# Two norms whose rows are transposed by a product with a diagonal of inverse roots

## The chip, the cores and the metric

The kernel runs on one NeuronCore of a Trainium2 chip. The metric is the device time of the core for one execution of the whole program, in microseconds (us). The time before is the median of three runs. The trace and the profile come from one further execution, taken with the hardware profiler.

## The reference, cut to what matters

Two blocks run one after the other on 256 tokens of 1024 columns, in float32. The first has two layers, each a mixer and a mixture of experts (MoE) with a layer norm behind either; the second begins with an RMS norm. What matters here is what stands behind each MoE:

```python
def layer_norm(x, g, b):
    mu = jnp.mean(xf, -1, keepdims=True)
    var = jnp.mean(jnp.square(xf - mu), -1, keepdims=True)
    return (xf - mu) * lax.rsqrt(var + LN_EPS) * g + b
...
    x = layer_norm(ALPHA * x + ffn, ln_ffn_g[l], ln_ffn_b[l])    # layer 0, then attention; layer 1, then second_block
...
def _rmsnorm(x, g):
    return xf * lax.rsqrt(jnp.mean(xf * xf, axis=-1, keepdims=True) + EPS) * g
...
    h = _rmsnorm(x, ln_mix_g[l])
    proj = h @ w_in[l]
```

Behind layer 0 the normed rows are multiplied by `w_kv` (keys and values) and `b_w_q`. Behind layer 1 they are normed once more (RMS) and multiplied by `w_in`.

## The kernel before

**Tiles.** The 256 tokens are two tiles of 128 (`t` in 0, 1), a token to a partition, with 1024 columns in `res`. A product wants its rows transposed: `x_hi` and `x_lo` hold eight chunks of 128 columns by 256 tokens. Every large product is made of three, x_hi·w_hi, x_lo·w_hi and x_hi·w_lo, in a rounded float32 type (`split_product`, L1726). ScalarE rounds the high halves of weights (`high`, L1185) and of rows out of the PSUM banks (`high_T`); VectorE, and at some places GpSimd, subtracts them to make the low halves (`low`, L704; `low_T`, L2642). Weights come through a ring of slots that SP fills, in order, as the slots come free; a block of weights is split in two halves (hb 0 and 1).

**Order.** Each engine has one list of instructions, written out by hand and followed in order; semaphores tell when an engine may go on (`ready`, `freed`, `claim`, `full`, `free` are waits and signals of the banks). GpSimd also issues small DMAs: the rows of gains and shifts and the table of attention bias.

**Behind an MoE** TensorE (PE) makes the last scatter products into four banks, then comes to a branch (L2175) that jumps over the code for experts with more tokens than they have slots for; this code is not taken with these inputs. VectorE adds the banks to `res` (`scattered`, L2983, its additions in L2992) and waits for its own four additions. Then the norm follows:

- `layer_norm_tok` (L2870) on VectorE: statistics of tile 0, then for each tile (row - mean) * gain into `xtok` (L2879), a reciprocal of the root (L2882) and xtok * root + shift (L2884). Gains and shifts are the rows `rows[1][:, 0, :]` and `rows[1][:, 1, :]`, loaded over all partitions.
- `second_tile` (L1206) on ScalarE: mean and variance of tile 1 by two passes with an accumulator, with `xtok` as scratch, and the roots. `root_ahead` (L1200) is a root of a constant that loads the root's table; it stands ahead of `second_tile` (L1391).
- First norm ("ln1", behind layer 0): PE makes two warming products (`warm`, L1720, product L1724) and transposes the rows (`norm_T`, L1927, call L2185, transposes L1936), chunk by chunk, tile 0 first. ScalarE rounds the banks to `x_hi`, VectorE makes `x_lo`, and the product with the first block of keys follows (`keys("k", 0)`, L2239), its first weights split ahead: both high halves by ScalarE at the end of the MoE (L1351), the first low half by GpSimd (L1100) and the second by VectorE behind `low_T` (L721). GpSimd waits for the normed rows (`ln1_tok`) before it loads the attention bias (L1103), since the bias lies where rows were.
- Second norm ("ln3" and then the RMS norm "rm0"): behind `layer_norm_tok` ScalarE squares the rows of each tile with an accumulator (L1521) and takes the root (L1524), VectorE a reciprocal (L2891) and a product (L2892) that writes the scaled rows to `res`, and PE, behind ten warming products, transposes them (call L2353).

The order of the three products in the first block of keys is unit by unit: four output chunks n, each with its three kinds of four products, in a half hb. The first block of the later MLP has a form of its own, `first_hidden` (L2563): all x_hi·w_hi of a half, then all x_lo·w_hi, then all x_hi·w_lo. The PE part `parameters` (L1857) waits for 12 parameter rows, transposes them, then waits for two rows of taps and transposes these. The MoE's experts run as PE L1940, ScalarE L1315, VectorE L2896, with `LAST` the last of eight pairs of experts.

Of the kernel before, what the change touches and what calls it, by code (L numbers as in the profile page):

```python
# [19 lines left out]
F32R = mybir.dt.float32r  # L20
# [5 lines left out]
P = 128  # L26
D = 1024
# [66 lines left out]
def program(nc, a, out):  # L94
    ctx = ExitStack()
    with ctx:
# [139 lines left out]
        parts = choice(NT, P)  # L236
        beats = choice(NG, PER_GROUP, PER_GROUP)
# [130 lines left out]
        ahead = tiny(8)  # L368
# [635 lines left out]
        def _(pool):  # L1004
# [95 lines left out]
            low(pool, g, FIRST_BEHIND[0], 0, pieces=4)  # L1100
# [36 lines left out]
        def _(act):  # L1137
# [68 lines left out]
            def second_tile(n):  # L1206

                at = int(n[2:]) // 2
                act.wait_ge(sem("res_whole"), at + 1)
                s.activation(xtok[:, 1, :], res[:, 1, :], ACT.Identity, accum_out=tile_sum).then_inc(sem("tile_sum"), 1)  # L1210
                std(n, eps_ln, (0,))
                act.wait_ge(sem("tile_sum"), at + 1)
                s.activation(mv[:, 1, 0:1], tile_sum, ACT.Copy, scale=1.0 / D).then_inc(sem("tile_mean"), 1)
                act.wait_ge(sem("tile_mean"), at + 1)
                s.activation(xtok[:, 1, :], res[:, 1, :], ACT.Square, scale=-1.0, bias=mv[:, 1, 0:1],
# [31 lines left out]
            for n in range(2):  # L1247
                par(wst[0:124, n, :], taps[n * 124:(n + 1) * 124, :], "par_taps")
# [66 lines left out]
            def experts(l):  # L1315
# [21 lines left out]
                for u in range(PAIRS):  # L1337
# [4 lines left out]
                    free(copy(hxT[:, 0, :, :], bank(("hT", l, u))[:].rearrange("p (j n) -> p j n", j=4)), ("hT", l, u))  # L1342
                    for r in rs[1:]:
                        gathered(u // 2 + 1, r)
# [6 lines left out]
                highs(FIRST_BEHIND[l])  # L1351
# [21 lines left out]
                with act.If(more > 0):  # L1373
                    over_pairs(act, over_copies)
                with act.Else():
                    act.sem_inc(sem("within"), 1)
# [14 lines left out]
            root_ahead()  # L1391
            second_tile("ln1")
            high_T("ln1")
# [120 lines left out]
            root_ahead()  # L1514
            second_tile("ln3")

# [189 lines left out]
        def _(pe):  # L1706
# [73 lines left out]

            def linear_tok(name, label, cols=HALF, i=0, **more):
# [75 lines left out]
            def parameters():  # L1857

                pe.wait_ge(sem("par_rows"), 16 * 12)
# [4 lines left out]
                pe.wait_ge(sem("par_taps"), 16 * 2)  # L1864
# [62 lines left out]
            def norm_T(name, src=res, made="xhat", before=0):  # L1927
# [257 lines left out]
            norm_T("ln1", xtok, "tok", 2)  # L2185
# [53 lines left out]
            keys("k", 0, arrives="ln1")  # L2239
# [1320 lines left out]
```

## Time and profile before

| what | value |
|---|---|
| median of three runs | 1200.62 us (1198.33 to 1203.09) |
| the profiled execution, its own time | 1205.38 us |
| its span in the trace | 1203.70 us |
| mean granted clock of TensorE, as a share of full speed | 0.989 |
| busy share of the span | PE 95%, weight load 66%, VectorE 53%, ScalarE 38%, GpSimd 19% |
| chain that ended last | PE 65%, VectorE 20%, DMA 5%, ScalarE 4%, issue 3% |

PE is TensorE's products and PEld its weight loads, which lie beside them; DVE is VectorE, ACT ScalarE, POOL GpSimd, SP SyncE. A name like L2992 is a line of the kernel. The chain is followed back from the last instruction, at each step to what released it; "issue" in it is time in which the engine waited for nothing that the profile shows. A row of a timeline gives start, busy time, engine, line, operation, output and inputs with their shapes, and in brackets how long the engine had been idle and what ended that.

### The profile page before, as it was taken

Reading aid. Unit: us, or ns where it says so; the run is one execution under the profiler, and the core shown is the slowest. Engines: PE = TensorE matmul, PEld = TensorE weight load, DVE = VectorE, ACT = ScalarE, POOL = GpSimd, SP = SyncE. Lnnn points to the kernel's source line nnn. Section 1 sums busy time; section 2 is a strip of 40 time slices with the busy share of each in tenths; the row PEclk is TensorE's granted clock in tenths of the full one; section 3 lists DMA queues with packets and bytes.
Section 4 is the critical chain, followed back from the end, with each engine's and each line's share of the span. In section 5 each row is a group of like instructions: output and inputs, shape, how many; then the busy total and the mean of one; then the engine's idle time right before and its main releaser. Section 6 shows DMA issues by size and latency. Waiting matters only on the chain.

```text
span 1203.7 us, 16471 instructions
## 1 busy us (share of the span) xinstructions
PE 1141.1 (95%) x6682; PEld 793.6 (66%) x6682; DVE 642.6 (53%) x969; ACT 453.5 (38%) x663; POOL 229.6 (19%) x198
## 2 busy tenths in 40 slices
PE   8999999999879998899999898999999889999998
PEld 8967544444239976444444347889887768998997
DVE  4897542222145767542222145873699885545544
ACT  4434411111034565411111025574566534443442
POOL 6500100000020000000000000586798541000000
PEclk9999999999989999999999999999999999999999
DMA  9497999999986447999999976443333342553550
GB/s 321 144 319 281 392 399 421 421 421 421 421 315 193 142 174 283 391 386 422 420 421 421 421 289 214 159 153 140 140 140 140 140 140 71 219 202 139 210 209 36
DMA packets 87222, 321.66 MB, mean 267 GB/s; under 512 B 7208, under 2 KB 18917, under 8 KB 62571
## 3 DMA queue, kind: packets, MB, share of 16 engines
q1 hardware_dynamic: 84336, 313.08, 67.3%
q0 software_dynamic: 2256, 7.30, 2.0%
q8 instruction: 54, 0.88, 0.3%
q10 hardware_dynamic: 554, 0.22, 0.1%
q14 instruction: 22, 0.17, 0.0%
HBM read 318.63 MB, written 1.96 MB: 266 GB/s over the span
## 4 chain that ended last, share of the span: by engine, by line
PE 65%; DVE 20%; DMA 5%; ACT 4%; issue 3%; POOL 2%; SPq 1%; DVEq 0%; ACTq 0%
PE bank L1764 30%; PE bank L2017 16%; PE bank L2087 8%; DMA arena<-in_moe_w_up_dram 5%; DVE w_lo L721 3%; ACT w_hi L1146 2%; PE bank L2099 2%; POOL w_lo L721 2%; DVE arena L2705 1%; PE bank L2008 1%; PE bank L2571 1%; PE bank L1808 1%; DVE arena L3020 1%; DVE arena L3364 1%; DVE rows L3345 1%
## 5 line engine op out<-in xcount | busy, mean ns | idle before, releaser
L1146 ACT ACTIVATE w_hi<-ring 128x2048 fp32r<-128x2048 f32 (+2 forms) x103 | 192.3, 1871 | 187.8 <-PE bank L1764 177.6
L721 DVE TENSOR_TENSOR w_lo<-ring,w_hi 128x2048 fp32r<-128x2048 f32 x71 | 161.9, 2282 | 135.2 <-ACT w_hi L1146 135.2
L721 POOL TENSOR_TENSOR w_lo<-ring,w_hi 128x512 fp32r<-128x512 f32 (+1 forms) x124 | 178.8, 1474 | 81.2 <-ACT w_hi L1146 81.2
L2017 PE MATMUL bank<-ring,moe_x 128*64 128x512 f32 x336 | 104.0, 610 | 7.4 <-DMA arena<-in_moe_w_up_dram 6.0
L1146 ACT ACTIVATE arena<-bank 128x512 f32<-128x512 f32 (+5 forms) x70 | 33.6, 492 | 203.9 <-PE bank L2074 184.3
L1764 PE MATMUL bank<-x_hi,w_hi 128*128 128x256 f32 (+1 forms) x616 | 101.8, 287 | 1.7 <-issue 1.7
L1764 PE MATMUL bank<-x_hi,w_lo 128*128 128x256 f32 (+1 forms) x616 | 99.4, 284 | 2.6 <-POOL w_lo L721 1.4
L1764 PE MATMUL bank<-x_lo,w_hi 128*128 128x256 f32 (+1 forms) x616 | 99.0, 283 | 0.5 <-DVE x_lo L2656 0.4
L1764 PE MATMUL bank<-w_hi,x_hi 128*128 128x512 f32 x320 | 91.7, 400 | 7.4 <-DVE x_lo L2787 2.9
L1764 PE MATMUL bank<-w_lo,x_hi 128*128 128x512 f32 x320 | 89.5, 393 | 4.2 <-POOL w_lo L721 3.5
L2981 DVE TENSOR_TENSOR y_r<-bank,y_r 128x512 fp32r<-128x512 f32 x32 | 22.1, 692 | 133.2 <-ACT y_r L1146 133.2
L1764 PE MATMUL bank<-w_hi,x_lo 128*128 128x512 f32 x320 | 88.7, 391 | 0.1
L1764 PEld LDWEIGHTS bank<-x_hi,w_hi 128*128 128x128 f32 (+1 forms) x616 | 84.5, 191 | 3.9 <-issue 3.3
L1764 PEld LDWEIGHTS bank<-x_hi,w_lo 128*128 128x128 f32 (+1 forms) x616 | 84.7, 191 | 3.2 <-POOL w_lo L721 1.8
L1764 PEld LDWEIGHTS bank<-x_lo,w_hi 128*128 128x128 f32 (+1 forms) x616 | 84.5, 191 | 1.1 <-issue 1.1
L2017 PE MATMUL bank<-arena,moe_x 128*64 128x512 f32 x240 | 82.5, 615 | 0.0
L3020 DVE SCALAR_TENSOR_TENSOR arena<-arena,small,bank 128x512 f32<-128x512 f32 x16 | 18.1, 1131 | 118.7 <-PE bank L2017 118.7
L1062 POOL DMA_DIRECT2D rows<-in_ln_ffn_g_dram x2 | 1.1, 536 | 392.8 <-DMA arena<-in_moe_w_down_dram 392.8
L2017 PEld LDWEIGHTS bank<-ring,moe_x 128*64 128x64 f32 x336 | 32.2, 140 | 65.7 <-issue 65.7
L1764 PEld LDWEIGHTS bank<-w_lo,x_hi 128*128 128x128 f32 x320 | 59.3, 188 | 20.4 <-POOL w_lo L721 7.0
L1764 PEld LDWEIGHTS bank<-w_hi,x_hi 128*128 128x128 f32 x320 | 58.2, 189 | 20.6 <-DVE x_lo L2787 3.8
L1764 PE MATMUL bank<-w_hi,mhT 128*128 128x512 f32 x256 | 70.1, 395 | 0.0
(409 smaller groups left out, 1827.4 us busy)
## 6 DMA issues: line engine op xcount, KB each, us to landing
ring<-in_moe_w_gate_dram SPq DMA_DIRECT2D x30, 1024.0 KB, 16.1
ring<-in_w_in_dram SPq DMA_DIRECT2D x15, 2048.0 KB, 7.6
arena<-in_moe_w_up_dram SPq DMA_DIRECT2D x26, 1024.0 KB, 19.1
arena<-in_moe_w_gate_dram SPq DMA_DIRECT2D x24, 1024.0 KB, 15.0
ring<-in_moe_w_up_dram SPq DMA_DIRECT2D x24, 1024.0 KB, 18.7
arena<-in_moe_w_down_dram SPq DMA_DIRECT2D x24, 1024.0 KB, 17.3
wslots<-in_moe_w_down_dram SPq DMA_DIRECT2D x24, 1024.0 KB, 21.4
ring<-in_w_mlp_up_dram SPq DMA_DIRECT2D x8, 2048.0 KB, 8.5
```

The lines of the kernel that those rows point to most:

```text
L721: last = ops.tensor_tensor(part(w_lo, label, hb)[:, x].bitcast(F32R), ring_half(label, hb)[:, x], part(w_hi, label, hb)[:, x], ALU.subtract)
L1146: return s.activation(dst, src, ACT.Copy)
L1764: last = mm(bank(use_)[0:still.shape[1], at:at + cols], still, moving, start=start and opens and (hb, n, k) == (0, 0, 0), stop=stop and cl ...
L1808: last = mm(bank(use_)[:, n % 2 * T:n % 2 * T + T], w_[hb][:, k, n * P:(n + 1) * P], x_[:, 4 * hb + k, :].bitcast(F32R), start=opens and n ...
L2008: last = mm(b[:, i * width:(i + 1) * width], rows_[:, t, c * P:(c + 1) * P].bitcast(F32R), sel[:, t, :].bitcast(F32R), start=(n, t) == (0, ...
L2017: last = mm(b[half * CAP:(half + 1) * CAP, :], still(k)[:, half * CAP:(half + 1) * CAP], moving(half, k), start=k == 0, stop=k == k_range - 1)
L2087: last = mm(bank(("y", l, u, h))[half * CAP:(half + 1) * CAP, :], hxT[:, 0, j, half * CAP:(half + 1) * CAP], down_rows(("down", l, 2 * u + ...
L2099: last = mm(b, sel_T[:, buf, t * P:(t + 1) * P].bitcast(F32R), y[:, h * HALF:(h + 1) * HALF].bitcast(F32R), start=n == 0, stop=n == 1)
L2571: last = mm(bank((*label, n // 2))[:, n % 2 * T:n % 2 * T + T], w_[hb][:, k, n * P:(n + 1) * P], x_[:, 4 * hb + k, :].bitcast(F32R), start ...
L2705: ins = v.scalar_tensor_tensor(conv[:, c, :], hpad[:, c, j:j + T], wdw[:, j * KD + c:j * KD + c + 1], conv[:, c, :], ALU.mult, ALU.add)
L2981: return v.tensor_tensor(y_lo[:, cols].bitcast(F32R), b, y_hi[:, cols], ALU.subtract)
L3020: free(v.scalar_tensor_tensor(hidden_rows(hx[:, 0, :]), by_hidden(sg[:, 0, :]), slot_gates[:, u % 2, :], by_hidden(bank(("up", l, u))[:]), ...
```

## The change

- **The two transposes.** `norm_T` gives way to `scaled_T`: a chunk of rows is not transposed as such but multiplied, in float32, by a diagonal matrix of inverse roots, so that the chunk comes out transposed and scaled. The diagonals lie in `scale_T` (the memory of `parts`), made by VectorE from the identity (`diagonal`). In the first norm the rows multiplied are (row - mean) * gain, and the shift comes into the banks before them, by 16 products of the shift's row with the identity that need nothing of the norm. One warming product in place of two goes ahead of these; in the second norm nine in place of ten.
- **The normed rows of the first norm**, which later work reads, are written behind the products' rows by `times_root`; GpSimd's wait for them stays.
- **VectorE's order.** It no longer waits for all four of the last additions together (`scattered`): tile 0's statistics wait for its own two banks, tile 1's product for the others. In the second norm both first products come ahead of both roots.
- **ScalarE's order.** `second_tile` waits for the banks instead of a signal of VectorE and uses `x_lo` as scratch. The root's table is asked for at the last pair of experts, behind the copy of `hT`; in the path for overfull experts it is asked for again. The second half of the split of the first weights goes behind `second_tile`.
- **The first low half** of the keys' weights goes from GpSimd to VectorE, behind `layer_norm_tok`.
- **The first block of keys** is multiplied in passes: `first_hidden` becomes `in_passes`, used for both.
- **Parameters and taps** count on one semaphore, waited for once.

```diff
+        scale_T = parts
...
-        ahead = tiny(8)
+        ahead = tiny(10)
...
-            low(pool, g, FIRST_BEHIND[0], 0, pieces=4)
             for t in range(NT):
                 pool.wait_ge(sem("ln1_tok"), t + 1)
             load_bias(0, bias1)
...
             def second_tile(n):
 
-                at = int(n[2:]) // 2
-                act.wait_ge(sem("res_whole"), at + 1)
-                s.activation(xtok[:, 1, :], res[:, 1, :], ACT.Identity, accum_out=tile_sum).then_inc(sem("tile_sum"), 1)
+                l = int(n[2:]) // 2
+                unread = x_lo[:, 0:4, :].rearrange("p c t -> p (c t)").bitcast(F32R)
+                for h in range(2):
+                    freed(act, ("sc", l, LAST, 1, h))
+                s.activation(unread, res[:, 1, :], ACT.Identity, accum_out=tile_sum).then_inc(sem("tile_mean"), 1)
+                act.wait_ge(sem("tile_mean"), 2 * l + 1)
+                s.activation(mv[:, 1, 0:1], tile_sum, ACT.Copy, scale=1.0 / D).then_inc(sem("tile_mean"), 1)
                 std(n, eps_ln, (0,))
-                act.wait_ge(sem("tile_sum"), at + 1)
-                s.activation(mv[:, 1, 0:1], tile_sum, ACT.Copy, scale=1.0 / D).then_inc(sem("tile_mean"), 1)
-                act.wait_ge(sem("tile_mean"), at + 1)
-                s.activation(xtok[:, 1, :], res[:, 1, :], ACT.Square, scale=-1.0, bias=mv[:, 1, 0:1],
+                act.wait_ge(sem("tile_mean"), 2 * l + 2)
+                s.activation(unread, res[:, 1, :], ACT.Square, scale=-1.0, bias=mv[:, 1, 0:1],
                              accum_out=mv[:, 1, 1:2]).then_inc(sem("ln_var"), 1)
...
-                par(wst[0:124, n, :], taps[n * 124:(n + 1) * 124, :], "par_taps")
+                par(wst[0:124, n, :], taps[n * 124:(n + 1) * 124, :], "par_rows")
...
+                    if u == LAST:
+                        root_ahead()
...
-                highs(FIRST_BEHIND[l])
+                high(FIRST_BEHIND[l], 0)
...
                     over_pairs(act, over_copies)
+                    root_ahead()
+                    act.wait_ge(sem(f"over_steps{l}"), 4 * PAIRS * (ROUNDS - 1))
...
             experts(0)
-            root_ahead()
             second_tile("ln1")
+            high(FIRST_BEHIND[0], 1)
             high_T("ln1")
...
+            def in_passes(label, arrives):
...
+                for hb in range(2):
+                    pe.wait_ge(hi_made[hb], nth_split(label) + 1)
+                    pe.wait_ge(sem("x_hi"), ROUNDED[arrives] + 2 * (hb + 1))
+                    for n in range(4):
+                        products(n, x_hi, wh, hb, opens=not hb)
+                    for b in (2 * hb, 2 * hb + 1):
+                        freed(pe, (arrives, b))
+                    for n in range(4):
+                        products(n, x_lo, wh, hb)
+                    pe.wait_ge(lo_made[hb], nth_split(label) + 1)
+                    for n in range(4):
+                        last = products(n, x_hi, wl, hb, closes=bool(hb))
+                        if n == 0:
+                            last.then_inc(hi_read[hb], 1)
+                        if hb and n % 2:
+                            full(last, (*label, n // 2))
+                    if not hb:
+                        last.then_inc(lo0_read, 1)
...
-                pe.wait_ge(sem("par_rows"), 16 * 12)
+                pe.wait_ge(sem("par_rows"), 16 * 14)
-                pe.wait_ge(sem("par_taps"), 16 * 2)
...
+            def scaled_T(name, before, shifted=False):
+
+                warm((name, 0), before)
+                for b in range(4):
+                    if b:
+                        claim(pe, (name, b))
+                    for c in (2 * b, 2 * b + 1) if shifted else ():
+                        for t in range(NT):
+                            at = c % 2 * T + t * P
+                            mm(bank((name, b))[:, at:at + P], rows[1][:, 1, c * P:(c + 1) * P], ident[:],
+                               start=(c % 2, t) == (0, 0), stop=False)
+                for t in range(NT):
+                    pe.wait_ge(sem("rows_scale"), NT * ("ln1", "rm0").index(name) + t + 1)
+                    for b in range(4):
+                        for c in (2 * b, 2 * b + 1):
+                            at = c % 2 * T + t * P
+                            last = mm(bank((name, b))[:, at:at + P], xtok[:, t, c * P:(c + 1) * P], scale_T[:, t, :],
+                                      start=not shifted, stop=not shifted or (c % 2, t) == (1, NT - 1))
+                        if t == NT - 1:
+                            full(last, (name, b))
...
             experts(0)
-            norm_T("ln1", xtok, "tok", 2)
+            pe.wait_ge(sem("rows1"), 32)
+            scaled_T("ln1", 1, shifted=True)
...
-            keys("k", 0, arrives="ln1")
+            in_passes(("k", 0), "ln1")
...
-            norm_T("rm0", before=10)
+            scaled_T("rm0", 9)
...
+            def times_root(n, t):
+                r = rows[1]
+                dve.wait_ge(sem(f"{n}_xhat"), t + 1)
+                v.scalar_tensor_tensor(xtok[:, t, :], xtok[:, t, :], rstd[:, t, 1:2], r[:, 1, :], ALU.mult, ALU.add)\
+                    .then_inc(sem(f"{n}_tok"), 1)
+            def diagonal(t):
+                v.tensor_scalar(scale_T[:, t, :], ident[:], rstd[:, t, 1:2], None, ALU.mult).then_inc(sem("rows_scale"), 1)
             def layer_norm_tok(n):
-                r = rows[1]
-                dve.wait_ge(sem("rows1"), 32 * (int(n[2:]) // 2 + 1))
-                for t in range(NT):
-                    if t == 0:
-                        half_stats(t, 0).then_inc(sem("res_whole"), 1)
-                        moments(n, t, half_stats(t, 1))
-                    dve.wait_ge(sem("ln_var"), NT * int(n[2:]) + t + 1)
+                l, r = int(n[2:]) // 2, rows[1]
+                dve.wait_ge(sem("rows1"), 32 * (l + 1))
+                def less_mean_gained(t):
                     v.scalar_tensor_tensor(xtok[:, t, :], res[:, t, :], mv[:, t, 0:1], r[:, 0, :], ALU.subtract, ALU.mult)\
                         .then_inc(sem(f"{n}_xhat"), 1)
+                def root(t):
                     dve.wait_ge(sem("ln_std"), NT * int(n[2:]) + t + 1)
                     link(v.reciprocal(rstd[:, t, 1:2], rstd[:, t, 0:1]))
-                    dve.wait_ge(sem(f"{n}_xhat"), t + 1)
-                    v.scalar_tensor_tensor(xtok[:, t, :], xtok[:, t, :], rstd[:, t, 1:2], r[:, 1, :], ALU.mult, ALU.add)\
-                        .then_inc(sem(f"{n}_tok"), 1)
-            def rms_norm(n):
+                    if n == "ln1":
+                        dve.wait_ge(sem(f"{n}_xhat"), t + 1)
+                        diagonal(t)
+                    else:
+                        times_root(n, t)
+                for h in range(2):
+                    freed(dve, ("sc", l, LAST, 0, h))
+                    last = half_stats(0, h)
+                moments(n, 0, last)
+                dve.wait_ge(sem("ln_var"), NT * int(n[2:]) + 1)
+                less_mean_gained(0)
+                if n == "ln1":
+                    root(0)
+                dve.wait_ge(sem("tile_mean"), 2 * l + 2)
+                for h in range(2):
+                    freed(dve, ("sc", l, LAST, 1, h))
+                less_mean_gained(1)
+                if n == "ln3":
+                    root(0)
+                root(1)
+            def rms_scale():
                 for t in range(NT):
                     dve.wait_ge(sem("rms_std"), t + 1)
                     link(v.reciprocal(rstd[:, t, 1:2], rstd[:, t, 0:1]))
-                    v.tensor_scalar(res[:, t, :], xtok[:, t, :], rstd[:, t, 1:2], None, ALU.mult)\
-                        .then_inc(sem(f"{n}_xhat"), 1)
+                    diagonal(t)
...
-                    for t in range(NT):
+                    for t in range(NT if u < LAST else 0):
...
             layer_norm_tok("ln1")
+            low(dve, v, ("k", 0), 0)
             low_T("ln1")
             low(dve, v, ("k", 0), 1)
+            for b in range(4):
+                ready(dve, ("ln1", b))
+            for t in range(NT):
+                times_root("ln1", t)
...
             layer_norm_tok("ln3")
-            rms_norm("rm0")
+            rms_scale()
```

## Rows read from the trace of the kernel before

**Rows 1.** Page, parts 1 and 3: busy time by engine; DMA queue 8, its packets, MB and share.

```profile
PE 1141.1 (95%) x6682; PEld 793.6 (66%) x6682; DVE 642.6 (53%) x969; ACT 453.5 (38%) x663; POOL 229.6 (19%) x198
...
q8 instruction: 54, 0.88, 0.3%
```

**Rows 2.** Chain of waits, 338 to 396 us: start us, us, what.

```profile
351.52 5.28 issue
356.80 3.75 PE bank L1724 x4
```

**Rows 3.** Line L2175: count, durations in ns (min/median/max), first and last start in us.

```profile
L2175 PEldq COMPARE_BRANCH  x2: 429/3344/6260, 350.4 to 712.8; - x2
```

**Rows 4.** DMA queues, 353.9 to 355.3 us: packets, MB, share of 16 engines.

```profile
q8 instruction: 1, 0.02, 4.9%
```

**Rows 5.** Windows: PE, PEld, DVE, ACT, POOL busy us (instructions), PE clock, DMA share, GB/s.

```profile
354.90:358.20 3.30, 1.40 (x2) 0.84 (x3) 3.27 (x3) 2.56 (x7) 2.41 (x2) 0.50 0.41 152
...
361.70:363.70 2.00, 1.31 (x12) 1.10 (x11) 0.71 (x2) 1.40 (x6) 1.30 (x2) 1.00 0.18 66
```

**Rows 6.** Timelines of VectorE and ScalarE, first norm: start us, us, instruction, idle before.

```profile
353.05 1.28 DVE L2663 BATCH_NORM_STATS2 stats<-res 128x6 f32<-128x512 f32 x2 [0.45 <-DVE res L2992]
...
359.70 1.28 DVE L2884 SCALAR_TENSOR_TENSOR xtok<-xtok,rstd,rows 128x1024 f32<-128x1024 f32 x1
...
362.30 2.32 ACT L1146 ACTIVATE x_hi<-bank 128x256 fp32r<-128x256 f32 x8 [4.78 <-PE bank L1936]
...
365.39 2.28 DVE L721 TENSOR_TENSOR w_lo<-ring,w_hi 128x2048 fp32r<-128x2048 f32 x1
```

**Rows 7.** Timeline of PE, second norm.

```profile
713.89 8.85 PE L1724 MATMUL bank<-blockmask,ident 128*128 128x512 f32 x20
```

**Rows 8.** Chain of waits, 700 to 752 us.

```profile
714.35 0.69 DVE res L2992
...
721.03 1.29 DVE xtok L2884
...
723.86 0.17 DVE rstd L2891
...
724.06 1.13 DVE res L2892
...
725.71 0.85 ACT x_hi L1154 x2
```

**Rows 9.** Line L2494: its PE instructions, and its first sixteen in the timeline.

```profile
L2494 PE MATMUL bank<-arena x128: 270/275/377, 843.6 to 940.8; 128*128 128x128 f32 x128
...
843.62 2.05 PE L2494 MATMUL bank<-arena 128*128 128x128 f32 x16 [1.12 <-DVE small L3352]
```

**Rows 10.** Timeline of PE, first norm.

```profile
360.34 2.57 PE L1936 MATMUL bank<-ident,xtok 128*128 128x128 f32 x16
...
363.61 0.71 PE L1764 MATMUL bank<-x_hi,w_hi 128*128 128x256 f32 x4 [0.69 <-issue]
...
364.42 0.71 PE L1764 MATMUL bank<-x_lo,w_hi 128*128 128x256 f32 x4
...
364.97 0.64 PE L1764 MATMUL bank<-x_hi,w_lo 128*128 128x256 f32 x4
```

**Rows 11.** Groups by line and form, VectorE: out<-in xcount | busy us, mean ns | idle before.

```profile
L3240 DVE TENSOR_SCALAR arena<-rows,small 128x128 f32<-128x128 f32 x1 | 0.3, 286 | 0.0
```

**Rows 12.** Timeline of ScalarE, first norm.

```profile
345.45 0.60 ACT L1146 ACTIVATE y_r<-bank 128x512 fp32r<-128x512 f32 x1 [3.90 <-PE bank L2087]
...
351.18 1.91 ACT L1146 ACTIVATE w_hi<-ring 128x2048 fp32r<-128x2048 f32 x1
353.10 1.28 ACT L1202 ACT_TABLE_LOAD   x1
```

**Rows 13.** DMA issues, 340 to 365 us: count, KB each, median us to landing.

```profile
arena<-bias_lines POOLq DMA_DIRECT2D x1, 1024.0 KB, 6.6
```

**Rows 14.** Timeline of VectorE, 389 to 392 us.

```profile
390.93 0.42 DVE L3087 SCALAR_TENSOR_TENSOR arena<-bank,arena 128x256 f32<-128x256 f32 x1
```

More of the change, by code:

```diff
@@ L1513, in _ @@
             experts(1)
-            root_ahead()
             second_tile("ln3")
+            high(FIRST_BEHIND[1], 1)
             def mean_square(n, arrived, of):
@@ L1779, in split_product, with products @@
                         last.then_inc(sem(blocks[label]["read"]), 1)
+            def in_passes(label, arrives):
+                wh, wl = ([part(w, label, hb).rearrange("p (k n) -> p k n", n=HALF).bitcast(F32R) for hb in range(2)]
+                          for w in (w_hi, w_lo))
+                def products(n, x_, w_, hb, opens=False, closes=False):
+                    for k in range(4):
+                        last = mm(bank((*label, n // 2))[:, n % 2 * T:n % 2 * T + T], w_[hb][:, k, n * P:(n + 1) * P],
+                                  x_[:, 4 * hb + k, :].bitcast(F32R), start=opens and (n % 2, k) == (0, 0),
+                                  stop=closes and (n % 2, k) == (1, 3))
+                    return last
+                for b in range(2):
+                    claim(pe, (*label, b))
+                for hb in range(2):
[16 more added lines that the diff above has]
+                        last.then_inc(lo0_read, 1)
             def linear_tok(name, label, cols=HALF, i=0, **more):
@@ L2561, in _ @@
             rows_T(1)
-            def first_hidden():
-                label = ("mu", 0)
-                wh, wl = ([part(w, label, hb).rearrange("p (k n) -> p k n", n=HALF).bitcast(F32R) for hb in range(2)]
-                          for w in (w_hi, w_lo))
-                def products(n, x_, w_, hb, opens=False, closes=False):
-                    for k in range(4):
-                        last = mm(bank((*label, n // 2))[:, n % 2 * T:n % 2 * T + T], w_[hb][:, k, n * P:(n + 1) * P],
-                                  x_[:, 4 * hb + k, :].bitcast(F32R), start=opens and (n % 2, k) == (0, 0),
-                                  stop=closes and (n % 2, k) == (1, 3))
-                    return last
-                for b in range(2):
-                    claim(pe, (*label, b))
-                for hb in range(2):
-                    pe.wait_ge(hi_made[hb], nth_split(label) + 1)
-                    pe.wait_ge(sem("x_hi"), ROUNDED["rm1"] + 2 * (hb + 1))
-                    for n in range(4):
-                        products(n, x_hi, wh, hb, opens=not hb)
-                    for t in range(NT):
-                        freed(pe, ("rm1", 2 * hb + t))
-                    for n in range(4):
-                        products(n, x_lo, wh, hb)
-                    pe.wait_ge(lo_made[hb], nth_split(label) + 1)
-                    for n in range(4):
-                        last = products(n, x_hi, wl, hb, closes=bool(hb))
-                        if n == 0:
-                            last.then_inc(hi_read[hb], 1)
-                        if hb and n % 2:
-                            full(last, (*label, n // 2))
-                    if not hb:
-                        last.then_inc(lo0_read, 1)
             OUT_ORDER = [(0, 0), (0, 1), (1, 0), (1, 1), (0, 2), (1, 2), (0, 3), (1, 3)]
@@ L2602, in mlp @@
                 if first:
-                    first_hidden()
+                    in_passes(("mu", 0), "rm1")
                 else:
@@ L2993, in scattered @@
                         free(ins, ("sc", l, u, t, h))
-                    for t in range(NT):
+                    for t in range(NT if u < LAST else 0):
                         for h in range(2):
```

## The prediction

> **What bounds the kernel now.** TensorE (PE) does: it is busy for 95% of the span [rows 1], so a norm between two stages costs what PE loses at it. I therefore read the chain of waits around the two norms that change, then each engine's timeline there.
>
> *First norm (behind the first MoE layer).* The reader should see that PE is not waiting for the norm when the stage begins. Its last scatter product ends at 351.52, and 5.28 us pass that the chain calls issue: PE waited for nothing that the profile shows. Two warming products and the transposes follow [rows 2]. The branch at L2175, which jumps over the code for overfull experts, says what it was: it took 6.26 us the first time and 0.43 us the second [rows 3]. Meanwhile a block of some 16 KB (54 blocks hold 0.88 MB) came over the instruction queue [rows 1, 4]. So this is a wait for code. Behind it the granted clock was 0.50 (1.2 GHz of 2.4), and at 361.7 it was back at 1.00 [rows 5]. VectorE's second tile ended at 359.70 + 1.28 = 360.98, and ScalarE began to round the new rows at 362.30 [rows 6].
>
> *Second norm (ahead of the second block).* Here PE's ten warming products run without a gap [rows 7], and the chain alternates between VectorE and ScalarE, from the end of the last addition at 715.04 to the first rounding at 725.71 [rows 8].
>
> By the Trainium skill's page Runtime: NRT & Kernel Launch, section Instruction fetch mechanics, a taken branch to a target outside the loaded window has to fetch that block first; the two times of this one branch agree with that.
>
> **The change, part by part.** Times are of the profiled execution: 1205.38 us, with a span of 1203.70. That is 4.8 us over the median of the three runs, 1200.62; the sum is made on the first and moved to the second.
>
> *The wait for code stays.* Ahead of that branch PE's program loses one wait at most (parameters and taps share a semaphore now), so branch and target move by one instruction out of some 250 in a block (6682 products, as many weight loads, 54 blocks [rows 1]). I take the 6.26 us as unchanged: PE begins at 356.80 as before.
>
> *What PE then does in the first norm.* Before: two warming products and 16 transposes. Now: one warming product, 16 float32 products that put the shift into the banks, 16 that multiply by the diagonal. A float32 product is two records: L2494's 64 products are 128. Sixteen records take 2.05 us, the last of them 0.28, so one starts every (2.05 - 0.28) / 15 = 0.118 us at full clock [rows 9], and every 0.236 at half. Warming: two records of (360.34 - 356.80) / 4 = 0.885 us [rows 2, 10], to 358.6. Shift: 32 records; 13.3 of them at half clock until 361.7, 18.7 more in 2.2 us, to 363.9. Tile 0: 16 records, 1.89 us, to 365.8. The first bank is whole after four records of tile 1, 3 x 0.118 + 0.28 = 0.63 us, at 366.4, where ScalarE begins instead of at 362.30: **+4.1 us**. The clock sets both ends: full speed throughout gives 356.80 + 0.89 + 3.78 + 1.89 + 0.63 = 364.0 (+1.7), half speed to the end 370.9 (+8.6). I take the value between, since up to 356.80 PE's history is that of rows 5.
>
> By the Trainium skill's page TensorE: Matmul & The Clock Gate, section Terms, transpose mode is four times faster for FP32; by that a product would cost four transposes and the first norm would lose some 7 us more. The rows show two records a product, and the sum goes by them.
>
> *What VectorE and ScalarE save there is covered.* VectorE begins its statistics with the end of the last addition, not 0.45 us later [rows 6], and no longer runs beside GpSimd's splitting. A multiply-add over 1024 columns gives way to a diagonal of 128 columns. The trace has no such diagonal; its ends are the 0.17 us reciprocal and the 1.13 us multiplication of 1024 columns [rows 8], and I take 0.29, a multiplication of 128 columns in SBUF [rows 11], as nearest. The second scale is then made at about 357.5, where the second tile was whole at 360.98. PE, which wants it at 365.8, hides all of that; without the wait for code it would count (rival 1).
>
> *Moved steps at no cost.* The root's table (1.28 us) goes into ScalarE's idle 3.90 us that end at 345.45; the second half of the split (1.91 us) goes behind the statistics, into the 4.78 us before 362.30 [rows 6, 12]. The low half of the first weight block passes from GpSimd to VectorE: 2.28 us [rows 6] between 357.5 and 366.4, where VectorE has nothing else; were PE ready at 358.8, the first low part of the rows would come 1 us late, which 16 products cover. The normed rows are written behind the products, 2 x 1.28 us on VectorE, whose next split has to wait for PE's last reading of the block and for ScalarE; without that cover, 2.6 us. GpSimd waits for these rows before it issues the bias load, which goes from 361 to about 374 and with 6.6 us in flight [rows 13] lands by 381; the row of shifts behind it in GpSimd's queue is read a layer later. The bias is first read at 390.93 [rows 14], and now later by the same shift: 10 us are left. SP's next weight load wants the low half read, and moves with PE. The joined wait for parameters and taps comes two small transposes earlier for the taps: 0.3 us at most, once.
>
> *First block in passes.* The same products in another order. The first group of four to the second took 0.81 us, against 0.55 for the next [rows 10]: **-0.3 us**, as the low part is wanted only after 16 products.
>
> *Second norm.* Statistics begin 0.45 us earlier. The new order (both first products, then both roots) has tile 0's rows whole at 720.5 and tile 1's at 721.9, where the latter were whole at 721.03 + 1.29 = 722.3. Square, sum and root took from there to 723.86, 1.54 us, and now end at 723.4; then a reciprocal (0.17) and a diagonal (0.29) stand for a reciprocal and a 1.13 us multiplication [rows 8], and the second scale is there at 723.9, not 725.2. But PE has tile 0 first: by the same steps its scale comes at 722.4, and 16 records take 1.89 us, to 724.3; then 0.63 us for the first bank: 724.9 against 725.71. **-0.8 us** (0 to -1.0 by the ends for the diagonal). What is late next is PE, no longer VectorE. Nine warming products instead of ten end before that.
>
> *Sum:* 4.1 - 0.3 - 0.8 = **+3.0 us**: 1208.4 for the profiled execution, **1203.6 us** on the median. What follows a norm shifts with it, the next MoE layer's loads too: SP issues them in order, as slots come free.
>
> **Rivals.**
> 1. *The wait for code goes* (the target is loaded in time, as at the second norm). PE then starts at 351.6 at full clock: 0.87 + 3.78 to 356.3, tile 0 to 358.2, the first bank at 358.8, and ScalarE begins 3.5 us earlier. With -0.3 and -0.8 that is -4.6: 1196.0 us. For it: the same branch took 0.43 us once [rows 3]. Against it: a single wait moves ahead of that branch. It decides where the first branch takes under some 2 us.
> 2. *The second branch gets a wait for code* (slower). Behind the first branch PE's program grows by 92 instructions (33 products of four against two of four and 16 transposes of two), so the second branch lies elsewhere in its block. Its price: 6.26 - 0.43 = 5.8 us, so warming starts at 719.7, at half clock; of 18 records 5.5 take 4.9 us, the rest 12.5 x 0.44 = 5.5 us, to 730.1; with 1.89 and 0.63 the first bank is whole at 732.6, 6.9 us late instead of 0.8 early. In all 4.1 - 0.3 + 6.9 = +10.7: 1211.3 us. It decides where the second branch takes over some 3 us. For it: the first branch. Against it: this jump once passed with room, and 92 of 250 need not use that up. By the section of the Trainium skill named above, Instruction fetch mechanics, it depends on nothing but the block in which the target falls.
> 3. *The clock stays at half* through the first norm's products: 8.6 - 0.3 - 0.8 = +7.5, 1208.1 us. Rows 5 speak against it.
>
> A table loaded again at the join behind the branch would change nothing: it was there before and is not in the chain of either norm.
>
> **How the numbers follow.** The forecast has 0.75, with 1201 to 1207 of its own by the clock; rival 1 has 0.13, rival 2 0.05, rival 3 0.04; 0.03 is left for what I don't see. A measurement of this kernel can tell about 0.5%, 6.0 us, from no change: faster is under 1194.6, slower over 1206.6. Rival 1 alone comes near the first, and with the runs' own spread of 2.4 us either way less than half of its chance falls below it; rivals 2 and 3 and the forecast's upper edge make slower. Faster 0.06, no change 0.81, slower 0.13. The range takes in the forecast with its clock and the runs' spread, and half of rival 1: 1196 to 1208.
>
> **What would show it.** Right: L2175 takes some 6 us first and under 1 us the second time; PE idles from 351.5 to 356.8 and then works without a gap through 64 records into about 366; VectorE has made the second scale before 358; ScalarE's first rounding falls at 366 in the first norm, and in the second 9.9 us behind the last addition (10.7 before). Wrong: a first rounding before 361, a long second branch, records of a product at other than 0.11 to 0.12 us.

## The result: 0.4% slower, and the profile after

| | before | after |
|---|---|---|
| median of six runs each | 1201.45 us (1198.33 to 1203.09) | 1207.76 us (1204.78 to 1209.28) |
| ratio | | 1.0042, 95% interval 1.0026 to 1.0058: 5.0 us slower (3.1 to 7.0) |
| profiled execution, its span | 1205.38, 1203.70 us | 1206.18, 1204.5 us |
| first norm: end of the last scatter product to ScalarE's first rounding | 351.52 to 362.30: 10.78 us | 350.70 to 364.96: 14.26 us |
| block of keys: its first product to that of the next block | 363.61 to 375.53: 11.92 us | 366.31 to 377.89: 11.58 us |
| second norm: end of the last addition to the first rounding | 715.04 to 725.71: 10.67 us | 717.23 to 728.93: 11.70 us |

The medians lie 6.3 us apart and the ratio on record makes it 5.0; its interval takes in both. The three stretches give +3.48, -0.34 and +1.03: +4.2 us, inside the interval too. The two profiled executions differ by 0.8 us only. In other stretches, with the same instructions in both, the granted clock fell at different places: from 97 to 100 us it was 0.50 after and 1.00 before, which cost PE some 1.6 us, and behind 1017 us it was the other way round, for 1.5 us. So the stretches are compared here, and the runs for the sum.

Busy time of the engines, part 1 of the page after [rows 1 of before]:

```profile
PE 1143.4 (95%) x6742; PEld 799.5 (66%) x6742; DVE 643.3 (53%) x972; ACT 453.5 (38%) x663; POOL 222.5 (18%) x194
```

PE has 60 records more: 46 in the first norm (66 against 20) and 14 in the second (50 against 36).

**First norm.** The branch's line, then the chain of waits of the kernel after [rows 2, 3]:

```profile
L2233 PEldq COMPARE_BRANCH  x2: 343/3385/6427, 349.6 to 715.0; - x2
```

```profile
350.70 5.60 issue
356.30 2.04 PE bank L1730 x2
358.34 4.34 PE bank L1986 x32
362.69 3.57 PE bank L1993 x32
366.26 0.05 issue
366.31 11.74 PE bank L1794 x96
```

The wait for code is there as before, 6.43 us at the first branch. Behind it PE works without a gap through one warming product (two records), 32 records of shift and 32 of rows. ScalarE begins to round when PE has filled the first bank (its timeline after):

```profile
364.96 2.32 ACT L1146 ACTIVATE x_hi<-bank 128x256 fp32r<-128x256 f32 x8 [8.15 <-PE bank L1993]
```

VectorE had both diagonals at 354.93 and 356.52, long before PE turned to the rows at 362.69 (its timeline after):

```profile
354.64 0.29 DVE L2905 TENSOR_SCALAR arena<-ident,rstd 128x128 f32<-128x128 f32 x1
...
356.23 0.29 DVE L2905 TENSOR_SCALAR arena<-ident,rstd 128x128 f32<-128x128 f32 x1
...
370.25 2.48 DVE L2900 SCALAR_TENSOR_TENSOR xtok<-xtok,rstd,rows 128x1024 f32<-128x1024 f32 x2
```

The windows of the kernel after give the clock [rows 5; columns as there]:

```profile
353.00:356.30 3.30, 0.00 (x1) 0.03 (x1) 3.19 (x7) 3.24 (x7) 0.00 (x0) 0.50 1.03 377
356.30:359.80 3.50, 3.50 (x10) 2.46 (x11) 2.42 (x2) 0.51 (x1) 0.00 (x0) 0.50 0.42 157
359.80:364.96 5.16, 5.16 (x48) 5.16 (x47) 0.00 (x0) 0.00 (x1) 0.00 (x0) 1.00 0.01 1
```

It fell while PE stood at the branch and was back 3.5 us behind PE's start; before, that took 361.7 - 356.8 = 4.9.

**Second norm.** VectorE's timeline after, then GpSimd's:

```profile
724.33 1.91 DVE L2905 TENSOR_SCALAR arena<-ident,rstd 128x128 f32<-128x128 f32 x1
725.52 0.72 DVE L2944 RECIPROCAL rstd<-rstd 128x1 f32<-128x1 f32 x1
726.30 0.29 DVE L2905 TENSOR_SCALAR arena<-ident,rstd 128x128 f32<-128x128 f32 x1
```

```profile
724.27 0.91 POOL L1098 DMA_DIRECT2D arena<-bias_lines  x1 [8.56 <-DVE xtok L2900]
725.18 0.97 POOL L1116 MEMSET arena<- 128x1024 f32 x1
```

The same instruction that took 0.29 us three times takes 1.91 here, and its end, 726.24, lies 0.09 us behind that of GpSimd's clearing (726.15). PE waits for it, and ScalarE for PE (their timelines, after):

```profile
716.09 7.99 PE L1730 MATMUL bank<-blockmask,ident 128*128 128x512 f32 x18
726.38 3.85 PE L1993 MATMUL bank<-arena,xtok 128*128 128x128 f32 x32 [2.30 <-DVE arena L2905]
...
728.93 3.03 ACT L1154 ACTIVATE x_hi<-bank,pcol 128x256 fp32r<-128x256 f32 x8 [3.44 <-PE bank L1993]
```

### The profile page after: what moved, and what is told of

It is laid out like the page before. It is cut to its first block, busy times and chain, and to the rows that moved or that the text cites. A ratio compares the mean times of both kernels' runs of the same rounds, so it can differ in the third digit from the quotient of the medians.

```text
span 1204.5 us, 16593 instructions
## 1 busy us (share of the span) xinstructions
PE 1143.4 (95%) x6742; PEld 799.5 (66%) x6742; DVE 643.3 (53%) x972; ACT 453.5 (38%) x663; POOL 222.5 (18%) x194
## 4 chain that ended last, share of the span: by engine, by line
PE 67%; DVE 17%; DMA 5%; ACT 4%; issue 3%; POOL 3%; SPq 0%; DVEq 0%; ACTq 0%
PE bank L1770 31%; PE bank L2075 16%; PE bank L2145 8%; DVE w_lo L722 3%; POOL w_lo L722 3%; DMA arena<-in_moe_w_down_dram 2%; DMA arena<-in_moe_w_up_dram 2%; ACT w_hi L1146 2%; PE bank L2157 2%; PE bank L1794 2%; DVE arena L2731 1%; DVE arena L3072 1%; PE bank L1846 1%; PE bank L2066 1%; DVE rows L3402 1%
## 5 line engine op out<-in xcount | busy, mean ns | idle before, releaser
L722 DVE TENSOR_TENSOR w_lo<-ring,w_hi 128x2048 fp32r<-128x2048 f32 (+1 forms) x72 | 164.1, 2282 | 131.9 <-ACT w_hi L1146 131.4
L722 POOL TENSOR_TENSOR w_lo<-ring,w_hi 128x512 fp32r<-128x512 f32 (+1 forms) x120 | 173.1, 1475 | 68.5 <-ACT w_hi L1146 68.5
L2075 PE MATMUL bank<-ring,moe_x 128*64 128x512 f32 x336 | 101.1, 600 | 7.9 <-DMA arena<-in_moe_w_up_dram 6.0
L1770 PE MATMUL bank<-x_hi,w_hi 128*128 128x256 f32 x584 | 96.6, 287 | 0.4 <-issue 0.4
L1770 PE MATMUL bank<-x_hi,w_lo 128*128 128x256 f32 x584 | 94.2, 284 | 2.6 <-POOL w_lo L722 1.4
L1770 PE MATMUL bank<-x_lo,w_hi 128*128 128x256 f32 x584 | 93.7, 283 | 0.3 <-DVE x_lo L2682 0.3
L1770 PEld LDWEIGHTS bank<-x_hi,w_lo 128*128 128x128 f32 x584 | 80.3, 191 | 3.2 <-POOL w_lo L722 1.8
L1770 PEld LDWEIGHTS bank<-x_hi,w_hi 128*128 128x128 f32 x584 | 80.1, 191 | 2.2 <-issue 1.7
L1770 PEld LDWEIGHTS bank<-x_lo,w_hi 128*128 128x128 f32 x584 | 80.1, 190 | 0.8 <-issue 0.8
L2075 PE MATMUL bank<-arena,moe_x 128*64 128x512 f32 x240 | 79.6, 601 | 0.0
```

Of the source, the lines that this page charges most:

```text
L722: last = ops.tensor_tensor(part(w_lo, label, hb)[:, x].bitcast(F32R), ring_half(label, hb)[:, x], part(w_hi, label, hb)[:, x], ALU.subtract)
L1770: last = mm(bank(use_)[0:still.shape[1], at:at + cols], still, moving, start=start and opens and (hb, n, k) == (0, 0, 0), stop=stop and cl ...
L2075: last = mm(b[half * CAP:(half + 1) * CAP, :], still(k)[:, half * CAP:(half + 1) * CAP], moving(half, k), start=k == 0, stop=k == k_range - 1)
```

## The experiments

Each kernel's norms are measured as in the table above. The kernel before has one more trace, that of before_clear_behind: its first norm, untouched there, took 10.00 us instead of 10.78. So one pair of traces doesn't show a difference under 1 us in the first norm. The second norm of the changed kernel (11.66 or 11.70 us in the five traces that leave its clearing as it is and have a short second jump) and its block of keys (11.58 or 11.59 in all eight traces with the passes) agree much better.

| kernel | ratio to before (95%) | median or single run, us | first norm | second norm |
|---|---|---|---|---|
| after | 1.0042 (1.0026 to 1.0058) | 1207.76 | 14.26 | 11.70 |
| after_placed | 0.9985 (0.9971 to 1.0000) | 1201.65 | 7.50 | 11.66 |
| before_placed | 1.0004 (0.9990 to 1.0018) | 1202.61 | 10.25 | 10.67 |
| after_no_shift | 1.0009 (0.9994 to 1.0023) | 1203.36 | 10.98 | 11.66 |
| after_second_far | 0.9999 (0.9986 to 1.0012) | 1201.19 | 6.97 | 15.37 |
| after_bias_behind | 1.0019 (1.0006 to 1.0032) | 1205.48 | 13.94 | 10.07 |
| after_clear_behind | single run | 1205.57 | 13.98 | 10.07 |
| before_clear_behind | single run | 1203.13 | 10.00 | 10.32 |
| after_units | single run | 1208.02 | 15.29 | 11.66 |
| placed_table_back | single run | 1200.93 | 7.74 | 11.66 |
| after_both | 0.9979 (0.9964 to 0.9993) | 1200.05 | 7.78 | 10.04 |

### The wait for code taken away, from either kernel

```diff
-            warm(("pw2", 0, 0), 4)
+            warm(("pw2", 0, 0), 18, cols=P)
...
                 with pe.If(more > 0):
+                    for _ in range(100 if l == 0 else 0):
+                        pe.sem_inc(sem("within"), 1)
```

after_placed has both edits on the kernel after, before_placed the first on the kernel before.

> The changed kernel with its program moved: 56 more instructions ahead of PE's first branch (18 short warming products ahead of the second convolution product instead of 4 long ones, in PE's idle time there) and 100 that are never executed behind it, so that both jumps land at other places of the program. Theory (the wait for code makes the first norm slower): both jumps take under 1 us, PE starts the warming product at most 0.5 us behind the last scatter product instead of 5.60 us, the 16 shift products end before the first diagonal, and ScalarE's first rounding falls 6.8 to 7.3 us behind the last scatter product instead of 14.26: some 7 us less, 1199 to 1201. Rival (the products themselves are the price): the first rounding stays over 10 us behind, and the time over 1203. Rival (the clock): PE works, but at half clock until the rounding, 9 to 11 us behind, 1202 to 1204.

> The kernel before with the same 56 instructions ahead of PE's first branch. Theory: the first jump takes under 1 us too, but VectorE's second tile (whole 9.46 us behind the last scatter product) then sets the end: first rounding 9.8 to 10.3 us behind instead of 10.78, 0.5 to 1 us less, about 1200.7. Rival (the wait for code cost the kernel before as much as the changed one): 5 us less, about 1196.

The branch's line in after_placed, then its timeline of PE:

```profile
L2233 PEldq COMPARE_BRANCH  x2: 404/430/455, 351.8 to 710.5; - x2
```

```profile
351.83 1.16 PE L2157 MATMUL bank<-y_r,selT_r 128*128 128x512 f32 x4 [0.37 <-DVE y_r L3035]
353.02 1.10 PE L1730 MATMUL bank<-blockmask,ident 128*128 128x512 f32 x2
353.95 3.73 PE L1986 MATMUL bank<-ident,rows 128*128 128x128 f32 x32
357.52 0.39 PE L1993 MATMUL bank<-arena,xtok 128*128 128x128 f32 x2
358.18 3.62 PE L1993 MATMUL bank<-arena,xtok 128*128 128x128 f32 x30 [0.27 <-issue]
```

Both jumps are short, and PE goes on 0.02 us behind its last scatter product. It turns from the shift to the rows at 357.52, and the first diagonal is there at 357.23, so PE and VectorE are about level. The norm takes 7.50 us instead of 14.26, and the ratio falls by 0.0057, 6.8 us: theory and size hold, though the time, 1201.65 us, lies a little over the 1199 to 1201 expected. The windows of the norm show a clock of 1.00 throughout:

```profile
353.00:353.90 0.90, 0.88 (x2) 0.47 (x3) 0.90 (x2) 0.00 (x0) 0.00 (x0) 1.00 1.05 382
353.90:357.50 3.60, 3.60 (x33) 3.55 (x32) 3.50 (x8) 3.27 (x8) 0.00 (x0) 1.00 0.96 354
357.50:360.50 3.00, 2.73 (x24) 2.54 (x23) 2.96 (x4) 1.60 (x2) 0.00 (x0) 1.00 0.14 46
```

In before_placed both jumps took under 0.46 us too, but PE then waits for VectorE (its timeline of PE):

```profile
351.41 1.98 PE L1724 MATMUL bank<-blockmask,ident 128*128 128x512 f32 x4
358.50 1.94 PE L1936 MATMUL bank<-ident,xtok 128*128 128x128 f32 x8 [5.10 <-DVE xtok L2884]
361.00 1.97 PE L1936 MATMUL bank<-ident,xtok 128*128 128x128 f32 x8 [0.56 <-DVE xtok L2884]
```

It idles 5.10 us, and the granted clock, back at 1.00 from 361.7 on in the kernel before, is 0.50 here from 358.4 until 367.0 (windows of before_placed):

```profile
363.03:367.00 3.97, 3.97 (x18) 3.97 (x19) 3.97 (x5) 2.50 (x6) 0.00 (x0) 0.50 0.88 316
367.00:372.00 5.00, 5.00 (x43) 5.00 (x43) 0.10 (x1) 1.58 (x1) 0.00 (x0) 1.00 0.92 287
```

The norm takes 10.25 us, which lies between the two traces of the kernel before (10.00 and 10.78), the block of keys behind it takes 13.34 instead of 11.92, and the time is that of the kernel before, not the 0.5 to 1 us less that were expected. So the old norm hid the wait for code behind VectorE, and the new one, which relieves VectorE and gives PE more to do, stands on it. Without that wait the change is worth 2.75 us in this norm, and in these two traces 1.75 more in the block of keys (13.34 to 11.59), most of it by the clock.

By the Trainium skill's page Runtime: NRT & Kernel Launch, section Instruction fetch mechanics, a taken branch waits for a fetch when its target lies outside the part of the program that is loaded. The four jumps of these two kernels agree: they took 0.32 to 0.46 us, with only the number of instructions ahead of them or skipped by them changed.

### The other branch made the far one

```diff
-                    for _ in range(100 if l == 0 else 0):
+                    for _ in range(20 if l == 0 else 0):
```

> As after_placed, but with 20 never executed instructions behind the first jump instead of 100, so that the second jump, and not the first, should land beyond the part of the program that is loaded. Theory (the wait for code goes by the place of a jump in the program alone): the first jump takes under 1 us and the second some 6 us; in the second norm PE's 18 warming records then begin about 5.5 us late and at half clock, and the first rounding falls about 17 us behind the last addition instead of 11.7; the time is 5 to 6 us over after_placed, 1206 to 1208. Rival (the second jump is always short, since more time lies before it): as after_placed.

The branch's line and the chain of waits of the second norm:

```profile
L2233 PEldq COMPARE_BRANCH  x2: 460/2345/4230, 347.3 to 705.4; - x2
```

```profile
706.54 3.26 issue
709.80 10.92 PE bank L1730 x18
720.72 2.25 PE bank L1993 x20
```

Against after_placed, where both jumps are short, eighty never executed instructions fewer bring a wait to the second jump; against the kernel after, the edits move the wait from one norm to the other. The jump took 4.23 us rather than 6, and the norm 15.37 us rather than 17. The time expected, 1206 to 1208 us, was missed: it was 1201.19. Against after_placed the two norms give +3.7 - 0.5 = 3.2 us; the ratio rose by 0.0014, 1.7 us, and each of the two ratios is uncertain by as much. That the wait goes by place is shown; why it was 2 us shorter here stays open.

### The shift left out

```diff
-            pe.wait_ge(sem("rows1"), 32)
-            scaled_T("ln1", 1, shifted=True)
+            scaled_T("ln1", 1)
```

This leaves the shift out of the rows from which keys, values and queries are made.

> The changed kernel without the 16 products that put the shift into the banks (the rows that the keys, values and queries are made of lack the shift). Theory (PE's list behind the wait for code sets the end of the first norm): PE idles 5.6 us as before, then 2 + 32 records, and the first rounding is 3 to 4.3 us earlier than 14.26 us behind the last scatter product; 3 to 4 us less. Rival (VectorE and ScalarE set the end): nothing changes.

The norm is 3.3 us shorter (14.26 to 10.98) and the ratio falls by 0.0033, 4.0 us. Behind its wait for code PE's own list is the path.

### GpSimd's work moved behind the diagonals

```diff
             pool.wait_ge(sem("ln3_tok"), NT)
+            pool.wait_ge(sem("rows_scale"), 2 * NT)
             load_bias(1, bias2)
```

In after_clear_behind the new wait stands behind `load_bias`, ahead of the clearing; in before_clear_behind it stands there too, on the scaled rows (`rm0_xhat`).

> The changed kernel, with one more wait on GpSimd: the second bias load and the clearing behind it wait for both diagonals of the second norm. Theory (GpSimd's load and clearing held up VectorE's first diagonal): that diagonal takes 0.29 us instead of 1.91 for the pair's first, the first rounding of the second norm falls 10.0 to 10.3 us behind the last addition instead of 11.7, and the time is 1.6 us less. Rival (the diagonal behind a reciprocal is itself so long there, or waits for ScalarE): it stays at over 1.5 us and nothing changes.

> The changed kernel with GpSimd's clearing (0.97 us) alone behind both diagonals of the second norm; the bias load stays ahead of them. If the load's issue (0.91 us on GpSimd, begun 0.06 us before the first diagonal) holds VectorE up as well, that diagonal ends with the issue, after 0.9 to 1.2 us; if the clearing alone does, it takes 0.29 us.

> The kernel before with GpSimd's clearing behind the second scaled rows of the second norm. Theory (the clearing held VectorE up there too, only less): the product of 1024 columns for the second tile takes 0.75 us, as the first tile's did, instead of 1.12, and the first rounding falls 10.3 us behind the last addition instead of 10.67. Rival (the second tile's product is itself longer): 1.12 us still.

VectorE and GpSimd in after_clear_behind (their timelines):

```profile
724.18 0.28 DVE L2906 TENSOR_SCALAR arena<-ident,rstd 128x128 f32<-128x128 f32 x1
...
725.57 0.29 DVE L2906 TENSOR_SCALAR arena<-ident,rstd 128x128 f32<-128x128 f32 x1
```

```profile
724.13 0.91 POOL L1098 DMA_DIRECT2D arena<-bias_lines  x1 [8.56 <-DVE xtok L2901]
725.92 0.95 POOL L1117 MEMSET arena<- 128x1024 f32 x1 [0.88 <-DVE arena L2906]
```

With the bias load beside it and the clearing behind, the first diagonal takes 0.28 us; the norm takes 10.07 us in both kernels, 1.63 less. So it is the clearing, not the load's issue. In the old kernel it cost 0.37: with the clearing behind, the second product took 0.75 us instead of 1.12, and the norm 10.32 instead of 10.67.

The lines of the kernel before, VectorE and GpSimd, then VectorE in before_clear_behind:

```profile
722.42 0.75 DVE L2892 TENSOR_SCALAR res<-xtok,rstd 128x1024 f32<-128x1024 f32 x1
...
724.06 1.12 DVE L2892 TENSOR_SCALAR res<-xtok,rstd 128x1024 f32<-128x1024 f32 x1
```

```profile
723.66 0.97 POOL L1116 MEMSET arena<- 128x1024 f32 x1
724.68 0.56 POOL L1118 MEMSET arena<- 128x16 f32 x1
```

```profile
721.82 0.75 DVE L2893 TENSOR_SCALAR res<-xtok,rstd 128x1024 f32<-128x1024 f32 x1
...
723.46 0.75 DVE L2893 TENSOR_SCALAR res<-xtok,rstd 128x1024 f32<-128x1024 f32 x1
```

It looks as if the hold goes both ways: beside the end of the long product GpSimd's second, small clearing took 0.56 us, and 0.12 us in before_clear_behind, where VectorE had nothing beside it. No run tried this by itself.

The ratio of after_bias_behind, 0.0023 under that of after (2.8 us), agrees with 1.63 us within the intervals.

### Two steps that were to cost nothing, or little

```diff
-            in_passes(("k", 0), "ln1")
+            keys("k", 0, arrives="ln1")
```

> The changed kernel with the first block of keys unit by unit again. Theory: from its first product to the first of the next block 11.9 us instead of 11.58, the first four products being followed by a gap until the first low part is there; 0.3 us more, too little for the time of a run. Rival: the passes make no difference, 11.6 us.

Unit by unit the block takes 11.92 us (367.04 to 378.96), as before; the passes are worth 0.34, as the theory had it. The run's first norm, 15.29 us, is the longest seen of the changed kernel: PE idled 5.66 us and the shift took 5.36 against 4.38 us, by the starts of the groups; that the units are the cause is not shown.

placed_table_back is after_placed with the calls of `root_ahead` back where the kernel before has them:

```diff
-                    if u == LAST:
-                        root_ahead()
...
+            root_ahead()
             second_tile("ln1")
```

> after_placed with the root's table asked for where the kernel before has it, ahead of the second tile's statistics. As PE waits for the diagonals here, this step no longer has the cover of the wait for code. Theory: ScalarE is idle for 1.40 us there, so the table's 1.28 us and the root of a constant, 0.20, make the statistics some 0.1 us later, and the first rounding about 7.6 us behind the last scatter product instead of 7.50; in the second norm, where ScalarE has only a short split ahead, nothing. Rival: the table's whole 1.28 us shows in either norm.

ScalarE's statistics begin 1.19 us behind the last scatter product, as against 1.17 in after_placed: the table was hidden even here. The norm's 7.74 us has another reason, a gap of 0.52 us within the records of tile 0, in place of 0.27, that the trace puts down to nothing. (after_second_far has no such gap, and its first norm took 6.97 us.)

### Both repairs

> The changed kernel with both repairs: its program moved as in after_placed, and GpSimd's second bias load and clearing behind both diagonals as in after_bias_behind. Theory (two separate losses, which add): first rounding about 7.5 us behind the last scatter product in the first norm and about 10.1 us behind the last addition in the second; 1.6 us less than after_placed, some 3.5 us under the kernel before (1198 to 1200 where that has 1202.4). Rival (the second norm's gain is taken up by what follows, PE or a weight load): no more than after_placed.

The first diagonal of the second norm takes 0.29 us, that norm 10.04 us, the first 7.78, with a gap of 0.56 us like that of placed_table_back. The ratio is 0.9979 (0.9964 to 0.9993): 2.5 us under the kernel before, where some 3.5 were expected, 7.6 under the changed one, and the lowest ratio here. Against after_placed the medians differ by 1.6 us, the size of the repair, though the intervals overlap.

## Why the prediction was right, step by step

- **The wait for code stays: right.** PE idled 5.60 us for 5.28, and the second jump stayed short (0.34 us). Rivals 1 and 2 did not come about in this kernel; both were made by moving the program alone, and rival 1's mechanism is what the change would need: 7.50 us for the norm, where the prediction's steps give 358.8 - 351.52 = 7.3. As a whole rival 1 was put at -4.6 us, and the ratio of after_placed gives -1.8; of the difference 1.8 us are the second norm, 1.0 longer there too instead of 0.8 shorter.
- **First norm, +4.1: the mechanism right, the size 0.6 too large.** It was +3.48 by the two traces, and the 0.6 is less than the 0.8 by which the kernel before's own two traces differ. The term that was off most is the shift, 5.3 us at two clocks by the prediction and 4.34 measured, since the clock was back 3.5 us behind PE's start and not 4.9. PE's start (5.60 us for 5.28) and the warming product (2.04 for 1.77) were 0.3 us off the other way. A float32 product is two records, and they start 0.11 to 0.12 us apart: 32 records take 3.73 us at full clock. A transpose is one such record (eight took 1.06 us in the second norm before), so a product costs two transposes and not four.
- **Second norm, -0.8: wrong, +1.03.** The step that failed is the diagonal at 0.29 us, "a multiplication of 128 columns in SBUF [rows 11], as nearest", with 1.13 us as its upper end. Its own cost was right (0.29 three times out of four), and so was what comes ahead of it: by the prediction's steps the first scale comes 722.4 - 715.04 = 7.4 us behind the last addition, and 724.33 + 0.29 - 717.23 = 7.4 is what it would have been without the hold. What the prediction left out is what runs beside it: GpSimd begins the bias load and its clearing with the end of tile 1's normed rows, and the diagonal comes 0.4 us behind these rows (723.97 to 724.33). With the clearing out of the way the norm takes 10.07 us against 10.67, -0.6, near the forecast; against the kernel before with its clearing out of the way too, 10.32, it is -0.25. The hint was in the trace before: the two products of one line, 0.75 and 1.12 us, were one instruction in two lengths; [rows 8] gave the longer, and only the longer was used.
- By the Trainium skill's page SBUF — State Buffer, section Who interferes with whom, a tensor_scalar of VectorE in a 2-port mode and GpSimd's work shut each other out, for the whole of an instruction; with that rule the clearing would have had to be priced. That VectorE is held to the clearing's end agrees; no row names the mode. By the same section of the Trainium skill the one that issues first goes first. The recorded starts, the diagonal's at 724.33 and the clearing's at 725.18, do not agree, but those of GpSimd are rough.
- **Passes, -0.3: right**, -0.34. **Table ahead, no cost and no gain: right**, also where the cover is gone. The low half on VectorE lay between 356.43 and 358.71, where VectorE had nothing else; the bias load went out at 373.28, behind the normed rows, and nothing waited for it.
- **The sum** was +3.0 against +5.0 (3.1 to 7.0) by the runs and +4.2 by the stretches: the direction was right, and so was that the change stays within 0.5%; the size was low by the 1.8 us of the second norm, less the 0.6 of the first. That these two errors have opposite signs is luck. By the medians the forecast was further off: 1207.76 lies 4.2 us over 1203.6, just under the upper edge of 1208. Of that 0.8 us is the kernel before, whose median was 1200.62 by three runs and 1201.45 by six. The 0.8 us between the stretches and the runs' ratio lie within its interval and were not traced further.

## What to carry to other kernels

When work is moved from a late engine to one that seems idle, look at what that engine's idle time is: here PE was waiting for its own program, and most of what was put behind that wait counted (the shift took 4.34 us, and leaving it out saved 3.3), while the same change with the program placed otherwise made the norm 2.75 us shorter (after_placed against before_placed). Two copies of one instruction that differ in length in the trace (0.75 and 1.12 us) ask for the engine that ran beside the longer. A few dozen instructions more, executed or not, can move a branch's target and with it a wait of 4 to 6 us, so the place of a branch is worth a look in every long program with jumps over unused code.

## What the runs showed of the hardware that was not expected

- GpSimd's clearing of 1024 columns (0.97 us) held a VectorE multiplication of 0.29 us for 1.91 us, though that had started 0.85 us before the clearing's recorded start; the issue of a DMA on GpSimd beside it (0.91 us) did not. Why the hold begins before the clearing's record does was not tried, and recorded times of GpSimd are rough.
- One jump over the same code took 0.32 to 0.46 us or 4.23 to 6.47 us, and the kernels made for it differ in nothing else near it than the number of instructions ahead of it or skipped by it.
- The granted clock stayed at 1.00 through a norm in which PE went on working (after_placed) and fell to 0.50 in the same norm where PE idled 5.1 us for VectorE or 5.6 us for its program: what is saved by having work for PE is also the products behind it at full clock. In before_placed the half clock lasted into the block of keys, which took 13.34 us instead of 11.92.
